# The last slot of each expert stage loaded in four pieces, with a semaphore for each

## What is computed

```python
he = silu(x @ wg[e]) * (x @ wu[e])          # wg, wu: 1024 x 512
y = y + gates[:, e:e + 1] * (he @ wd[e])    # wd: 512 x 1024
```

## Time and profile before

| | |
|---|---|
| Median of three runs | 1106.36 us (1096.42 to 1106.67) |
| Span of the profiled execution | 1107.2 us |
| TensorE busy | 992.3 us, 90% of the span |
| VectorE, ScalarE, GpSimd busy | 348.4, 216.9, 134.4 us |
| Mean rate of the DMA engines | 270 GB/s |
| Slot loads | 138 of 2 MB, median 12.6 us from issue to landing |
| Down product (L576) | 114.4 us busy, 608 matmuls |

### The profile page before, as it was taken

How to read it: one execution, slowest core, us unless ns; L and a number is a source line. 1 busy time by engine, 2 the same in 40 slices (tenths; PEclk the granted TensorE clock), 3 DMA queues, 4 the chain that set the end, 5 groups by cost and what they waited for, 6 DMA issues and landing times. The chain is left out here.

```text
span 1107.2 us, 13949 instructions
## 1 busy us (share of the span) xinstructions
PE 992.3 (90%) x5538; PEld 568.3 (51%) x5538; DVE 348.4 (31%) x820; ACT 216.9 (20%) x513; POOL 134.4 (12%) x149
## 2 busy tenths in 40 slices
PE   7899998898899898979999998899698989898986
PEld 3344456764333333337787677588586323333334
DVE  1101125248101010123333767678427400101004
ACT  2110045132101000103333521213103200000003
POOL 1000000000000000001000266575001000000000
PEclk9899999899989999989999999999798999999998
DMA  9995782064999999994655400222234699999991
GB/s 377 406 408 220 315 310 77 29 244 188 401 427 428 429 427 426 428 427 172 236 220 191 190 1 1 76 76 77 77 113 191 262 411 426 426 428 429 428 382 38
DMA packets 22443, 299.48 MB, mean 270 GB/s; under 512 B 2592, under 2 KB 2720, under 8 KB 4320
## 3 DMA queue, kind: packets, MB, share of 16 engines
q1 hardware_dynamic: 20880, 292.45, 64.4%
q0 software_dynamic: 1488, 6.03, 1.4%
HBM read 295.32 MB, written 3.15 MB: 270 GB/s over the span
## 5 line engine op out<-in xcount | busy, mean ns | idle before, releaser
L558 PE MATMUL bank<-ring,arena 128*32 128x512 f32 (+1 forms) x1216 | 200.1, 598 | 7.5 <-DMA ring<-slots 7.5
L576 PE MATMUL bank<-ring,arena 128*32 128x512 f32 (+1 forms) x608 | 114.4, 685 | 34.1 <-DMA ring<-slots 29.0
L558 PEld LDWEIGHTS bank<-ring,arena 128*32 128x32 f32 (+1 forms) x1216 | 60.9, 123 | 142.6 <-issue 132.6
L832 DVE TENSOR_TENSOR arena<-arena,bank 128x256 f32<-128x256 f32 x28 | 11.8, 421 | 300.9 <-ACT arena L661 300.9
L986 PE MATMUL bank<-act_t,ring 128*128 128x256 f32 x384 | 89.5, 387 | 2.0 <-DVE act_t L442 2.0
L1540 PE MATMUL bank<-ring,act_t 128*128 128x512 f32 x192 | 87.2, 607 | 3.2 <-DVE act_t L1805 2.4
L576 PEld LDWEIGHTS bank<-ring,arena 128*32 128x32 f32 (+1 forms) x608 | 32.3, 135 | 97.1 <-issue 87.2
L986 PEld LDWEIGHTS bank<-act_t,ring 128*128 128x128 f32 x384 | 72.3, 193 | 16.3 <-issue 4.2
L899 POOL COPY arena<-arena 128x512 f32 (+1 forms) x34 | 17.5, 515 | 384.9 <-PE bank L558 306.1
L916 PE MATMUL bank<-act_t,ring 128*128 128x256 f32 x256 | 61.2, 402 | 1.6 <-ACT act_t L1278 0.9
L1540 PEld LDWEIGHTS bank<-ring,act_t 128*128 128x128 f32 x192 | 36.0, 193 | 51.2 <-issue 46.4
(11 more groups left out here) (325 smaller groups left out, 1290.1 us busy)
## 6 DMA issues: line engine op xcount, KB each, us to landing
ring<-slots SPq DMA_DIRECT2D x138, 2048.0 KB, 12.6
cst<-consts SPq DMA_DIRECT2D x1, 1260.5 KB, 36.5
act_t<-x_t POOLq DMA_DIRECT2D x1, 1024.0 KB, 12.7
ring<-state POOLq DMA_DIRECT2D x1, 1024.0 KB, 5.1
out_st<-arena POOLq DMA_DIRECT2D x4, 256.0 KB, 4.1
out_y<-arena SPq DMA_DIRECT2D x4, 256.0 KB, 2.1
par<-params SPq DMA_DIRECT2D x1, 613.0 KB, 3.9
arena<-nat_bias POOLq DMA_DIRECT2D x1, 512.0 KB, 22.1
```

The lines of the kernel that those rows point to most:

```text
L558: last = pe.matmul(bk[to:to + wide, :], x[:, 4 * m + c, wide * e:wide * e + wide], w[:, c, 512 * t:512 * t + 512], start=(m == 0 and c == ...
L576: last = pe.matmul(bank[3][to:to + wide, :], ht[:, col + wide * e:col + wide * e + wide], w[:, f, 512 * t:512 * t + 512], start=(f == 0), ...
```

## The change

The last place of each expert stage is loaded by four DMAs of 512 KB, one for each of the four blocks of 1024 columns that the steps of `down` read. The first three add 16 to `part0`, `params_or_part1` and `consts_or_part2`, the fourth to the slot's own `slot_full`. The second and third are the semaphores of the parameter and constant loads under new names; their counts go on from 16, so that the expert stages wait for 16 more. In `down`, the block that holds rank 15 leaves out the wait ahead of its first step and waits ahead of each step for that step's piece. The same is done in both plans and both stages. To make room for one more semaphore, `dot_banks_free` is gone with its wait on TensorE and its signal on ScalarE. The places left out of the diff below are the same two renames.

```diff
--- before.py
+++ after.py
@@ -41,6 +41,7 @@
 
 FIXED = (4, 5)
 FIXED_CAP, FIXED_SLOTS = 32, 64
+LAST_PARTS = ("part0", "params_or_part1", "consts_or_part2")
 UNITS = ((0, 1), (8, 9), (2,), (5,), (10, 11), (3,), (6,), (12, 13), (4,), (7,), (14, 15))
 SEQ = [(r, m) for unit in UNITS for m in range(3) for r in unit]
 LEAN_CAP = (FIXED_CAP,) * 2 + (128,) * 3 + (64,) * 3 + (32,) * 8
@@ -566,9 +567,14 @@
                 wide = 64 // len(parts)
                 ws = []
                 for r, at in parts:
-                    k = wait_slot(pe, n0, SEQ.index((r, 2)))
+                    at_seq = SEQ.index((r, 2))
+                    k = at_ring(n0, at_seq)[0] if at_seq == 3 * N_EXP - 1 else wait_slot(pe, n0, at_seq)
                     ws.append(ring[:, k, :].rearrange("p (f n) -> p f n", f=FC))
                 for f in range(FC):
+                    if parts[-1][0] == SEQ[-1][0] and f < FC - 1:
+                        pe.wait_ge(S(LAST_PARTS[f]), 16 * (L + 1 + (f > 0)))
+                    elif parts[-1][0] == SEQ[-1][0]:
+                        wait_slot(pe, n0, 3 * N_EXP - 1)
                     col = (f % 2) * P + (f // 2) * 64
                     for e, w in enumerate(ws):
                         for t in range(2):
@@ -1156,8 +1162,6 @@
                                             o_d[:, s, c * P:(c + 1) * P], ident)
                     last.then_inc(S("dot_done"), 1)
             pe.wait_ge(S("dot_copied"), 4)
-
-            pe.wait_ge(S("dot_banks_free"), 1)
             out_pe(pe, 1, OOUT0)
 
 
@@ -1278,8 +1282,6 @@
                     act.activation(act_t[:, 4 * q:4 * q + 4, s * P:(s + 1) * P],
                                    bank[2 * s + q][:, :].rearrange("p (h n) -> p h n", h=4), ACT.Copy,
                                    scale=p_("onorm")).then_inc(S("dot_copied"), 1)
-            act.wait_ge(S("dot_copied"), 4)
-            act.sem_inc(S("dot_banks_free"), 1)
 
         def delta_pool(pool, ch):
             pool.memset(zpad, 0.0).then_inc(S("pad_zero"), 1)
@@ -1529,7 +1531,7 @@
 
         @block.tensor
         def _(pe):
-            pe.wait_ge(S("params_in"), 16)
+            pe.wait_ge(S("params_or_part1"), 16)
             pe.wait_ge(S("cond_ready"), 1)
 
             def project(n, c0, c1):
...
@@ -1900,12 +1902,12 @@
 
         @block.sync
         def _(sp):
-            sp.dma_start(par[:, :], params).then_inc(S("params_in"), 16)
+            sp.dma_start(par[:, :], params).then_inc(S("params_or_part1"), 16)
             sp.dma_start(ident, consts[:, 0:P]).then_inc(S("ident_or_y"), 16)
             for k in range(RING):
                 sp.dma_start(ring[:, k, :], slots[k]).then_inc(slot_full[k], 16)
                 if k == ADA_FIRST:
-                    sp.dma_start(cst[:, P:N_CONST], consts[:, P:N_CONST]).then_inc(S("consts_in"), 16)
+                    sp.dma_start(cst[:, P:N_CONST], consts[:, P:N_CONST]).then_inc(S("consts_or_part2"), 16)
             for pos in range(RING, N_SLOTS):
                 k = pos % RING
                 if pos == SCRATCH:
@@ -1925,7 +1927,13 @@
                         at = sp.value_load(flags[0:1, 0, r:r + 1], min_val=0, max_val=3 * N_EXP - 3)
                     row = at + (n0 + m - (n0 > SCRATCH))
                 sp.wait_ge(slot_free[k], pos // RING)
-                sp.dma_start(ring[:, k, :], slots[bass.ds(row, 1)].rearrange("a p n -> (a p) n")).then_inc(slot_full[k], 16)
+                src = slots[bass.ds(row, 1)].rearrange("a p n -> (a p) n")
+                if layer is not None and pos == n0 + 3 * N_EXP - 1:
+                    for f in range(FC - 1):
+                        sp.dma_start(ring[:, k, f * D:(f + 1) * D], src[:, f * D:(f + 1) * D]).then_inc(S(LAST_PARTS[f]), 16)
+                    sp.dma_start(ring[:, k, (FC - 1) * D:FC * D], src[:, (FC - 1) * D:FC * D]).then_inc(slot_full[k], 16)
+                    continue
+                sp.dma_start(ring[:, k, :], src).then_inc(slot_full[k], 16)
             for g in range(4):
                 q, s = g // 2, g % 2
                 sp.wait_ge(S("y_ready"), g + 1)
```

More of the change, by code:

```diff
@@ L1577, in _ @@
             ada_columns(pe, ADA_PROJ - 1, bank[6])
-            pe.wait_ge(S("consts_in"), 16)
+            pe.wait_ge(S("consts_or_part2"), 16)
             pe.wait_ge(S("proj_copied"), 12)
@@ L1686, in _ @@
             ch = Chain(act, "act_step")
-            act.wait_ge(S("params_in"), 16)
+            act.wait_ge(S("params_or_part1"), 16)
             act.activation(p_("cond"), p_("cond"), ACT.Silu).then_inc(S("cond_ready"), 1)
@@ L1786, in _ @@
             dve.memset(idle_w, 0.0).then_inc(S("idle_ready"), 1)
-            dve.wait_ge(S("params_in"), 16)
+            dve.wait_ge(S("params_or_part1"), 16)
             for i, name in enumerate(("ln_g", "ln_b")):
@@ L1943, in _ @@
             pool.wait_ge(S("even_in"), 112)
-            pool.wait_ge(S("consts_in"), 16)
+            pool.wait_ge(S("consts_or_part2"), 16)
             pool.tensor_tensor(bias, bias, ec_("window").unsqueeze(1).to_broadcast([P, 8, P]), ALU.add).then_inc(S("bias_ready"), 1)
```

## The result

The changed kernel takes 1097.67 us (median of 20 runs, 1091.46 to 1108.42) against 1107.47 us (20 runs, 1096.42 to 1115.22). The ratio of the two, for which executions over 1.5% above the fastest of their kernel are left out, is 0.9931: 7.6 us less, with a 95% interval of 0.9912 to 0.9950 (5.5 to 9.7 us). The medians lie 9.8 us apart, just outside that interval. The forecast was 1097.3 us with a range of 1087 to 1102.5, and "within 1%" as the likeliest outcome; both hold. That the median comes within 0.4 us of the forecast is partly luck. The profiled execution has a span of 1093.2 us (its own time 1094.96), 14.0 us under the span of before, more than the medians' difference.

The account below looks back on a forecast made before the run. The weight stream sets the time in the two expert stages, so work behind each last landing counts. Gains of 5.12 and 3.97 us, 9.1 in all, take the median 1106.36 to 1097.3 us, range 1087 to 1102.5.

Parts of the forecast that it names:

- What bounds the end: Both expert stages' ends: the last down product starts 0.1 us behind the last landing; only work left after it counts.
- The sum: Both expert stages' ends: gains of 5.12 us in the first and 3.97 us in the second, 9.1 us in all.
- Its two halves: Last down products: 4.6 us from steps moved ahead of the last landing, 4.5 us from the clock not falling.
- clock rival: Last down products: clock falls despite short pauses, steps take 1.7 us, gain 5.0 us, 1101.4 us; chance 0.12.
- The price of short rows: Last slot's loads: 4 KB instead of 16 KB rows cost 0.3 us a stage, bounds 0 and 0.6 us.
- Pieces that don't overlap: Last slot of either stage: each piece pays its own delay, landing 6.1 us later, 1110.6 us; chance 0.04.
- no gain: Last slot: pieces finish together or one late engine holds all four back, 1106 to 1106.5 us; chance 0.08.
- laggard: Last slot's loads: one DMA engine of sixteen is behind for the wait's last 2 us, supposedly carrying an instruction packet.
- Extra issues and waits at nothing: SyncE and TensorE at stage ends: three more issues (about 1 us) and three more waits per stage cost nothing.
- 13.4 to 14 us from the issue: Last slot of each stage: the landing, counted from the issue, stays at 13.4 to 14 us.
- The handshake at nothing: DeltaNet's end: removing ScalarE's signal and TensorE's wait gives 0 us, bounds 0 and 0.1 us.
- More than the tails: Selection after the first stage: a clock fall is missed, 3.3 us more gain, 12.4 us in all, 1094.0 us; chance 0.20.

Follow-up runs that it names:

- kernel without the handshake: Kernel before with only ScalarE's signal dot_banks_free and TensorE's wait for it removed; 1109.8 us, ratio 1.0041.
- kernel with one wait: Changed kernel, but TensorE waits for all four pieces ahead of the first step; 1104.7 us, ratio 1.0005 to the kernel before.
- filled wait: Kernel before with matmuls of constants ahead of each stage's last down product; five: 1103.8 us, ratio 1.0002; four: 1101.2 us (one run).
- kernels with 160 and 64 instructions more: Changed kernel with 160 or 64 instructions added in the first stage's untaken branch; 1100.0 us (ratio 0.9924) and 1104.8 us (one run).

## Why the prediction was right

- **What bounds the end.** Right. In the changed kernel each step waits for its piece, and TensorE ends 1.1 us behind the last landing instead of 6.6 and 5.5.
- **The sum.** The forecast was 5.12 and 3.97 us, 9.1 in all; the two profiled executions give 5.30 and 4.37, 9.7 in all; the ratio says 7.6 (5.5 to 9.7), the medians 9.8. The forecast took the tails from one execution. With a fall of the clock as short as in the kernel without the handshake (9.97 and 9.61 us copy to copy) the same change would give 4.0 us a stage, 8.0 in all (my estimate). So it was partly luck that the one execution it went by was near the others.
- **Its two halves.** The kernel with one wait loses both together. The filled wait tells them apart: the clock's share is 2.8 of 2.83 us where it could be read, and the steps' share in a stage the 2.7 us from there to the changed kernel, less 0.2 us for the shorter rows, 2.5 us where the forecast had 2.3. The clock rival (a fall all the same, 1101.4 us) is out: no step in the profiles of the kernels with four pieces and four waits took over 1.1 us.
- **The price of short rows.** Taken at 0.3 us between 0 and 0.6, it is 0.2; for 2 KB rows, whose price came from the output's stores, 0.45 instead of 0.6.
- **Pieces that don't overlap, and no gain.** Both out, by the landings: the pieces of the first stage were complete at 478.2, 479.5, 480.7 and 482.0, each with its own late share 1.5 to 1.6 us behind the other fifteen. The laggard held each piece back and not all of them to the end.
- **Extra issues and waits at nothing.** Right: the last piece was issued at 1057.81, 11.8 us ahead of its landing. The sign "13.4 to 14 us from the issue" was loosely put: from the first piece's issue the last lands 13.8 and 13.4 us later, from its own 12.2 and 11.8. After the first stage the next stage's first product still follows VectorE, 18.8 us behind the result's copy as before.
- **The handshake at nothing.** Its idle time is the same; the time of the kernel without it alone is not explained, and the kernel with one wait, which lacks the handshake too, shows no such loss.
- **More than the tails.** The rival at 0.20 named the selection, and in the profiled execution it came true (3.75 against 7.06 us). The second profile of the changed kernel has 7.06 us again, and so have the kernels with 160 and 64 instructions more; kernels made from the one before have 7.06 (no handshake) or 3.76 (matmuls in the wait). I take it for a draw and not a part of the change.
- **What was wrong.** The pause before the first step was forecast at 0.5 to 1 us; it is 0.77 us in the first stage and nothing in the second, where TensorE wasn't ready before 1065.8. And I counted a step's matmuls as one after the other when I expected something of half steps.

## What to carry to other kernels

In a stage that its weight stream bounds, only what is left to do behind the last byte counts: order the last load's consumer so that most of it needs only earlier bytes, and give each part its own semaphore. Ask whether a long wait also costs the clock, since here that was half of the gain, and two pieces would already have saved it. Read such a change off the landing and the product's end in single traces, because whole executions of one kernel lay up to 11 us off their median here, and most of 12.5 us between two of them was the clock in places that have nothing to do with the change.

## What was not expected of the hardware

- TensorE's own code comes through the DMA engines that carry the weights: packets of 16 KB, about every 20 us in the stages, moved when code was put ahead of them. In the cases followed here a packet held one of a slot's sixteen shares back by some 1.5 us, and those of the slots after it too. Where that share was among the late ones already, the last slot's sixteenth share came 0.7 to 2.3 us behind the fifteenth; where it was an early one, nothing was lost (0.06 us).
- Four float32 matmuls that write to four groups of 32 output rows started together, within 0.02 us (1069.65 to 1069.67); two of them took as long as four (1.1 us from landing to end in both cases).
- Two executions of one kernel differ by 12.5 us of span at mean clocks of 0.958 and 0.972: 9 us of it in one stretch where TensorE was busy almost throughout in both, at a granted clock of 0.62 in one and 1.00 in the other.
